# Eight tiled rotary score products a group in the sample attention, and the next scores ahead of the last values in the prompt attention

## The reference, cut to what matters

```python
def _attn_block(q_lat, q_pe, q_pos, ckv, kpe, k_pos):
    s = (jnp.einsum('bqhl,bkl->bhqk', q_lat, ckv, preferred_element_type=jnp.float32)
         + jnp.einsum('bqhr,bkr->bhqk', q_pe, kpe, preferred_element_type=jnp.float32))
    mask = (k_pos[None, :] <= q_pos[:, None])[None, None]
    s = jnp.where(mask, s * MLA_SCALE, NEG_INF)
    p = jax.nn.softmax(s, axis=-1).astype(ckv.dtype)
    return jnp.einsum('bhqk,bkl->bqhl', p, ckv)
```

## Time and profile before

| | us |
|---|---|
| median of 3 runs (lowest, highest) | 3275.3 (3270.05, 3279.39) |
| the profiled execution: its time | 3277.29 |
| the profiled execution: its span, first to last instruction | 3275.6 |
| units of the prompt attention, layer 0 and layer 1 | 207 and 215 |
| sample attention from its first `flip`, layer 0 and layer 1 | 208 and 201 |

### The profile page before, as it was taken

One profiled execution on the slowest core, in us unless ns is written; L12 is line 12 of the kernel. 1 busy time (PEld: TensorE's weight loads), 2 busy tenths in 40 slices (PEclk: granted clock), 3 DMA queues, 4 the chain that ended last, 5 costly groups with the idle time before them and its releaser, 6 DMA issues. The chain is left out here.

```text
span 3275.6 us, 50941 instructions
## 1 busy us (share of the span) xinstructions
PE 3079.1 (94%) x20834; PEld 2741.3 (84%) x20834; DVE 1806.3 (55%) x3092; ACT 924.3 (28%) x1486; POOL 244.0 (7%) x280
## 2 busy tenths in 40 slices
PE   6987898998999999999989779989989999999998
PEld 5965576667999999999989546766689999999998
DVE  4856676554454454544565756755535454544544
ACT  4034443443321111111220444434423111111113
POOL 2000001540000000000020000025300000000000
PEclk8986999998999999999989879999989999999999
DMA  4112001663021111111031310036521111111112
GB/s 102 46 38 60 16 4 41 234 219 93 14 71 39 38 54 42 58 39 39 22 54 34 65 41 5 2 131 219 169 67 38 47 52 45 58 38 38 53 31 71
DMA packets 226528, 207.03 MB, mean 63 GB/s; under 512 B 50260, under 2 KB 195796, under 8 KB 226148
## 3 DMA queue, kind: packets, MB, share of 16 engines
q1 hardware_dynamic: 200744, 119.38, 13.4%
q0 software_dynamic: 25600, 85.11, 8.4%
HBM read 193.58 MB, written 11.05 MB: 62 GB/s over the span
## 5 line engine op out<-in xcount | busy, mean ns | idle before, releaser
L189 PE MATMUL ps<-streamH,upH 128*128 128x344 f32 x2112 | 448.4, 321 | 0.0
L189 PE MATMUL ps<-streamH,upL 128*128 128x344 f32 x2112 | 447.2, 320 | 0.0
L189 PE MATMUL ps<-streamL,upH 128*128 128x344 f32 x2112 | 445.9, 319 | 0.0
L2253 ACT ACTIVATE upH<-hc 128x1024 fp32r<-128x1024 f32 x88 | 93.4, 1061 | 959.8 <-PE ps L189 959.8
L189 PEld LDWEIGHTS ps<-streamH,upL 128*128 128x128 f32 x2112 | 355.9, 188 | 0.0
L189 PEld LDWEIGHTS ps<-streamH,upH 128*128 128x128 f32 x2112 | 354.7, 188 | 0.7
L189 PEld LDWEIGHTS ps<-streamL,upH 128*128 128x128 f32 x2112 | 352.7, 188 | 0.0
L2417 DVE TENSOR_TENSOR xT<-xT,ps 128x1032 f32<-128x1032 f32 x176 | 215.9, 1228 | 227.6 <-PE ps L189 227.6
L443 PE MATMUL ps<-inH,inW 128*128 128x344 f32 (+1 forms) x1248 | 234.1, 323 | 31.1 <-DVE inW L497 31.1
L2378 DVE TENSOR_TENSOR hc<-ps,rstd 128x1032 f32<-128x1032 f32 x44 | 54.2, 1232 | 362.8 <-PE ps L189 362.8
L443 PEld LDWEIGHTS ps<-inH,inW 128*128 128x128 f32 (+1 forms) x1248 | 198.9, 183 | 38.3 <-DVE inW L497 32.1
(11 more groups left out here) (468 smaller groups left out, 4969.9 us busy)
## 6 DMA issues: line engine op xcount, KB each, us to landing
hc<-in_w_ffn_in SPq DMA_DIRECT2D x88, 512.0 KB, 4.4
hc<-in_w_ffn_out SPq DMA_DIRECT2D x44, 512.0 KB, 3.7
big<-in_w_in SPq DMA_DIRECT2D x22, 512.0 KB, 4.5
stream_raw<-in_w_out SPq DMA_DIRECT2D x16, 512.0 KB, 3.8
big<-in_x_prompt SPq DMA_DIRECT2D x2, 2048.0 KB, 10.1
out_y_prompt<-big SPq DMA_DIRECT2D x8, 512.0 KB
scratch_y<-hc SPq DMA_DIRECT2D x16, 136.0 KB, 3.3
scratch_u<-wring SPq DMA_DIRECT2D x4, 516.0 KB, 3.1
```

What stands on the lines that cost most here:

```text
L189: last = pe.matmul(self.ps[:, bank + n, 0:NCOL], w, x[:, n * NCOL:(n + 1) * NCOL], start=(k == 0 and i == 0), stop=(k == len(terms) - 1 an ...
L2253: act.activation(upH[u][:, :, :], raw[u], ACT.Copy).then_inc(g_wh[u], 1)
```

## The change

In the prompt attention two lines of PE's loop change places. In the sample attention the rotary part is made of eight products of a 32x32 block of weights, four for each half c, all ahead of the latent part of half 0; `qr32` holds the queries of one sample in 32 columns, in all four blocks of 32 partitions; the block of partitions that a product reads is `row_tile(c, i)`, which is i for c = 0 and (i + 2) mod 4 for c = 1. So that the keys lie there, `reorder` swaps the first and the last two samples in tiles 4 to 7, in three ACT instructions in place of one. At the start of the stage DVE makes `qr32` with one copy where it made `qrq` with eight.

```diff
@@ mla_prompt, PE
                     transposes(u)
+                    if u + 2 < NU:
+                        scores(u + 2)
                     if u >= 1:
                         values(u - 1)
-                    if u + 2 < NU:
-                        scores(u + 2)
@@ mla_sample
-        qrq = W(256, 2 * P).rearrange("p (z x) -> p z x", z=2)
+        qr32 = W(256, SAMPLES * 32)
+        def row_tile(c, i):
+            return (i + 2 * c) % 4
@@ PE
+                def rotated_scores(g):
+                    z = g % 2
+                    if g >= 1:
+                        pe.wait_ge(f_p, g)
+                    cleared(pe, order["rot", g, 0])
+                    for c in range(2):
+                        for i in range(4):
+                            b, at = 4 * z + i, row_tile(c, i) * ROPE
+                            pe.matmul(ps[32 * i:32 * i + 32, S_BANK + c, :], qr32[at:at + ROPE, 32 * b:32 * b + 32],
+                                      rtb[at:at + ROPE, c * 512:(c + 1) * 512], start=True, stop=False)
+
                 def scores(g, c):
                     z = g % 2
-                    if g >= 1 and c == 0:
-                        pe.wait_ge(f_p, g)
-                    cleared(pe, order["rot", g, 0])
-                    pe.matmul(ps[:, S_BANK + c, :], qrq[:, z, :], rtb[:, c * 512:(c + 1) * 512], start=True, stop=False)
+                    if c == 0:
+                        rotated_scores(g)
                     cleared(pe, order["lat", 2 * g + c, 1])
@@ ACT, reorder
-                    act.activation(rord.rearrange("p (t b c) -> p t b c", b=4, c=ROPE), keys, ACT.Copy).then_inc(f_rl, 1)
+                    turned = rord.rearrange("p (t b c) -> p t b c", b=4, c=ROPE)
+                    act.activation(turned[:, 0:4], keys[:, 0:4], ACT.Copy)
+                    act.activation(turned[:, 4:8, 0:2], keys[:, 4:8, 2:4], ACT.Copy)
+                    act.activation(turned[:, 4:8, 2:4], keys[:, 4:8, 0:2], ACT.Copy).then_inc(f_rl, 1)
@@ DVE, start of the stage
-                for b in range(SAMPLES):
-                    z, i = b // 4, b % 4
-                    rows = slice(ROPE * i, ROPE * i + ROPE)
-                    dve.tensor_copy(qrq[rows, z, 32 * i:32 * i + 8], self.qr[rows, b, :])
+                dve.tensor_copy(qr32.rearrange("p (b x) -> p b x", x=32)[:, :, 0:8], self.qr)
```

More of the change, by code:

```diff
@@ L1946, in _ @@
                 s = Steps(dve, f_dve)
-                for t in (q32, qrq, selT, own):
+                for t in (q32, qr32, selT, own):
                     last = dve.memset(t, 0.0)
```

## The result

| | us |
|---|---|
| before, median on the same chip (lowest, highest) | 3277.15 (3270.05, 3279.39) |
| changed, median (lowest, highest) | 3235.89 (3227.78, 3239.89) |
| ratio, with its 95% interval | 0.9875 [0.985, 0.9899] |
| profiled execution: its time and its span | 3235.72 and 3234.1 |

A forecast was written before the change was run, and what follows sets the result against it. PE, busy 94% of the span, was taken as the bound: its work in the sample attention, work plus small waits in the prompt attention. 3277.3 less 23 less 17 gave 3237 us; own range 3222 to 3251, 8-in-10 range 3219 to 3263.

The forecast's parts named there:

- The tiles, 23 us: Sample attention, rotary products on PE: a group's sum falls from 3.70 to 2.98 us, 23 us over 32 groups.
- The second rival: Sample attention: the two tiles of a column block take turns, 3 us lost instead of 23 won, 3263 us; chance 0.06.
- The rival of the shared bank: Sample attention: a half's four tiles, writing one bank, follow each other, 58 us lost, 3318 us; chance 0.10.
- The swap, 17 us: Prompt attention: scores before values shorten PE's waits at transposes (18.5 us, 15.0 taken) and step (2.3 taken); bounds 0 to 24.
- The step of the argument that put two or three waits a layer out of reach: Prompt attention, transposes: waits of the third and last units stay, their scores having no or few values ahead; 3.5 us.
- The step's waits: Prompt attention: of PE's 5.6 us in 6 waits at a step, 6 x 0.39 = 2.3 us would go.
- The setup, counted at nothing: Sample stage start: one DVE copy for eight saves 1.2 us a layer, but PE waits for gathered pages; 0 to 2.4.
- `reorder`, counted at nothing: Sample attention, ACT: three instructions add 0.29 us a group, 9 us in all, hidden under PE's work.
- the strictest rival: Sample attention: tiles sharing a bank take turns and PE starts strictly in order, 139 us, about 3400; bank turns' chance 0.10.

## Why the prediction was right

**The tiles, 23 us: right, term by term.** 0.96, 1.02 and 1.03 stand where 0.96, 1.00 and 1.02 were worked out. The 28 full groups save 0.71 each, 19.9 together, and the first and last groups, by the same rows, an estimated 3.5 more. The stretch shows 20.8 because of what happens at its two ends, which the prediction left out. Its first five `flip`s, up to the first rotary product, take 7.1 and 7.2 us after 5.9 and 6.0. They come sooner after the gap between the stages, in which PE mostly waits, and so more of them run at a granted clock of 0.50, the 1.2 GHz level, which lasts to 581.6 before and to 570.1 in the changed kernel (layer 0). First the kernel before, then the changed one:

```profile
578.72 3.33 PE L1817 MATMUL ps<-cst,big 128*128 128x128 f32 x16 [0.58 <-DVE wring L1972]
581.88 1.04 PE L1817 MATMUL ps<-cst,wring 128*128 128x128 f32 x8
```

```profile
565.07 3.68 PE L1821 MATMUL ps<-cst,big 128*128 128x128 f32 x16 [0.58 <-DVE wring L1985]
568.54 1.80 PE L1821 MATMUL ps<-cst,wring 128*128 128x128 f32 x8
```

That is 2.3 us in the two layers. PE also waits 2.2 for gathered pages, where the trace before has one wait of 0.35. Some 1.5 come back at the end of the stretch, where less of the work falls into the next time at 0.50.

The second rival's course does occur, but only where two tiles share one part of the array (12.00 a group). The rival of the shared bank is refuted: each bank is written by four tiles of different rows, and sixteen records last 1.09. The rule that spoke for it (the Trainium skill, TensorEngine Tiling (Array Packing), Gotcha 1) is that such tiles cannot use one bank at the same time; this trace does not agree with it, where every tile writes partitions of its own.

**The swap, 17 us: the mechanism was right, the size low; 22.1 measured.** At the transposes 17.4 of 18.5 went, where I kept 15.0. The step of the argument that put two or three waits a layer out of reach failed. The third unit's wait stayed, as said (0.56 at 366.4), but those of the last units went, such as this one of the kernel before:

```profile
558.34 0.98 PE L1452 MATMUL ps<-cst,big 128*128 128x128 f32 x7 [1.05 <-ACT big L1541]
```

The step's waits gave 2.6 for 2.3. One new wait came, 0.44 a layer, of values for ACT's `output`. The other 3 us or so are no wait: in the units of layer 0 (windows of 208 us before, 197 after, with the same 1187 products) PE's idle time fell from 14.1 to 4.9, which is what its listed waits lost, and its busy time from 193.87 to this:

```profile
361.00:558.00 197.00, 192.10 (x1187) 149.57 (x1187) 149.55 (x406) 87.18 (x231) 7.68 (x8) 1.00 0.07 19
```

That this is records overlapping more where no wait parts them is my reading, not tested.

**The setup, counted at nothing: about right in the sum, by another way than the one given.** I took the gathered pages to be what PE waits for first. An earlier product waits for DVE behind the copies, and the head shortened by 3.6 in two layers, more than the 2.4 that I set as its bound. The 2.3 of the slower first `flip`s and the 1.9 of longer waits for pages take that back. That they follow from the shorter head is read from the runs, whose heads of 9.2, 8.0 and 7.5 us (layer 0) go with first `flip`s of 5.9, 7.0 and 7.1; no run changes the head alone by more than 0.5 us.

**`reorder`, counted at nothing: right.** Its pieces took 0.62, 0.41 and 0.41 each where I estimated 0.60, 0.37 and 0.37 (ACT's timeline), and no wait of PE on them appeared:

```profile
642.45 0.62 ACT L1928 ACTIVATE wring<-wring 128x512 f32<-128x512 f32 x1
642.97 0.41 ACT L1929 ACTIVATE wring<-wring 128x256 f32<-128x256 f32 x1
643.27 0.41 ACT L1930 ACTIVATE wring<-wring 128x256 f32<-128x256 f32 x1
```

**That the total came within 1 us is luck.** Left out of the sum was the shift of the feed-forward's code, which costs 7.5 us. The swap's missing 5, the 1.5 at the end of the groups and 2.5 of small changes elsewhere, whose cause I did not look for, make up for it. Two figures are a little off without bearing on this: by its own terms the forecast's range begins at 3220 (3277.3 - 33 - 24), not 3222, and the strictest rival loses 141 us, not 139.

## What to carry to other kernels

In this case small products of 32 rows and 32 columns of weights ran side by side where no two shared one 32x32 part of the array (eight in 1.09 us, 1.92 where they met in pairs), and laying the second set in rotated rows was worth extra instructions on an engine with time to spare. Where an in-order engine waits for a chain on other engines, start that chain before the work that feeds nothing urgent. Added instructions can cost time in a loop that comes later, so compare the stages that the change doesn't touch, and the packets of the instruction queue, before the gain is put down to the edit.

## What the runs showed of the hardware

The feed-forward's loop ran either without loading code or with it, by its place alone. In the kernel before the instruction queue has no packet from 1060 to 1460 us; in the changed one it has this, and PE pauses about once a pass, every 137.5 us (136.1 before):

```profile
q8 instruction: 24, 0.39, 0.4%
```

```profile
1041.08 0.73 PE L189 MATMUL ps<-streamH,upH 128*128 128x344 f32 x3 [1.00 <-issue]
...
1178.63 0.74 PE L189 MATMUL ps<-streamH,upH 128*128 128x344 f32 x3 [1.15 <-issue]
...
1316.12 0.73 PE L189 MATMUL ps<-streamH,upH 128*128 128x344 f32 x3 [1.10 <-issue]
```

Layer 1 has three such pauses too; the view of waits puts the last of them (1.35 at 2906.9) down to DVE.

Those 400 us hold 2.9 passes, so a pass loads about 8 packets of 16 KB (3.03 MB in 185). In the trace 1,765 PE instructions lie between one jump back and the next: 864 products, 864 loads of weights and 37 others. The Trainium skill (Runtime: NRT & Kernel Launch, Instruction fetch mechanics) says that instructions are fetched in blocks of 16 KiB, 256 instructions, that PE's store holds 2,048 of them, and that a jump out of the current two blocks stalls. The packets' size agrees, and so do the offsets, 0 and 512 against 112 and 368. That the kernel before jumps back over 1,765 instructions without any load agrees with the 2,048 and not with two blocks. An estimate with the 256 of the Trainium skill (the same section): 1,765 instructions are 6.9 blocks, so by where the loop begins it touches seven or eight. That seven stay and eight do not would fit all runs here, but the loop's own place in the code is in no trace, so the reason is not shown. Which offsets between 0 and 256 keep the loop resident was not tried.
